# Which engine subtracts the gate weights, when the last quarter loads, and two spare products

## The chip, the cores and the metric

The kernel runs on 1 core of one Trainium2 chip. The metric is device time in microseconds; the runs shown are three executions of the kernel before, with the median as its time.

## The reference, cut to what matters

One decoder layer: 512 tokens, width 1024, all float32. The part that the change touches is the very end, after the mixture of experts:

```python
ffn = _hierarchical_moe(x, ...)                    # per token: two chosen experts
x = _layer_norm(DEEPNORM_ALPHA * x + ffn, ln2_g, ln2_b)
return x + jax.nn.sigmoid(x @ ple_gate_w) * (p_i @ ple_proj_w)
```

`ple_gate_w` is 1024 x 1024, `ple_proj_w` 256 x 1024.

## The kernel before, in words

Each engine has a hand-written program of its own; semaphores order them. A float32 product of full precision is made of three fast ones: weights and activations are each split into a rounded high part (`fp32r`, made by ScalarE with a copy) and the remainder, the low part (a subtraction: raw minus high). TensorE then does high x high, high x low and low x high (`three`, lines 1944 to 1948).

Up to about 560 us the experts run, one item after another: 41 items in all. GpSimd gathers their tokens and scatters their results to DRAM (`pair_dram`). What follows is the epilogue, the functions named `rest` of each engine:

- SyncE (lines 668 to 684) waits until all scattered results have landed, then loads each tile's two rows of expert results ("the pairs", 512 KB for each of tile and choice, `pair_of(t)`), for the four token tiles t of 128, in order, and in between the last two quarters of the gate weights. The gate weights come in four quarters of 1 MB: quarter q holds half `q // 2` of the output columns and half `q % 2` of the contraction. Quarters 0 and 1 are loaded earlier (line 628).
- ScalarE (`rest` from line 1188): rounds quarters 0 and 1 (`round_gate`, line 1161), copies the eight results of the embedding product out of PSUM (`ple_out`, line 1124), rounding quarter 2 after the sixth; waits for two low quarters (line 1195); then for each tile rounds the transposed rows (`turned_high`, line 1200, two halves); rounds quarter 3 after tile 0's; later the sigmoids (line 1207).
- VectorE (`rest` from line 1894): `split_gate(0)` and `split_gate(1)` (line 1858: 128 x 2048 elements, raw minus high); then for each tile t two `expert_sum` (line 1901, result row times its weight plus the residual, 128 x 1024), between them the low parts of the tile before (`turned_low`, line 1602), statistics (line 1577), variance (lines 1583, 1585), `norm_centre` (line 1589) and `norm_scale` (line 1596); `split_gate(2)` after tile 0's scaling and `split_gate(3)` after tile 1's; last the eight products and additions (lines 1934, 1936).
- GpSimd (`rest`, line 895): for each tile `inverse` (line 818), one power of 128 x 1 elements: it waits for the variance, and `norm_scale` waits for it.
- TensorE (`rest` from line 2431): the embedding product (`embed`, line 2228, full float32, 16 products that the profile counts as 32), two spare products whose result nobody reads, the transposition of tile 0 (line 2217, two halves of four), five more spare products, and then the gate products (`gate(t, q)`, 12 fast products for each quarter q and tile t) in the order (0,0) (0,1) (0,2), transposition of tile 1, (0,3) (1,0) (1,1) (1,2), transposition of tile 2, and so on. `gate(0, 0)` needs the first low half of tile 0 (`s_x2lo`); `gate(0, q)` needs the low part of quarter q (`s_glo` at q + 1). The spare products keep TensorE busy; line 2269 is theirs.

Semaphores of the change: `s_ghi` counts rounded quarters, `s_glo` low quarters, `s_quarter[q]` the landing of quarter q, `s_ve2` variances, `s_rs2` inverse roots, `s_ln2` steps of the normalisation, `s_pev` copies of the embedding product, `s_mix` the last products and additions.

Of the kernel before, what the change touches and what calls it, by code (L numbers as in the profile page):

```python
# [4 lines left out]
F32 = mybir.dt.float32  # L5
# [3 lines left out]
ALU = mybir.AluOpType  # L9
# [6 lines left out]
NT, NK = SEQ // P, DM // P  # L16
# [82 lines left out]
def hybrid_layer(nc, d, out, x1_dram, pair_dram):  # L99
    ctx = ExitStack()  # L100
    with ctx:
# [3 lines left out]
        def sem(name):  # L105
            return ctx.enter_context(nc.semaphore(name))
# [51 lines left out]
        bank = [ctx.enter_context(nc.psum_tensor(f"bank{i}", [P, 512], F32)) for i in range(8)]  # L158
# [151 lines left out]
        gate_raw = pieces[SLOTS] + [y_flat[:, 0:GW]]  # L310
        gate_hi = [w_hi[:, GW:2 * GW], w_hi[:, 2 * GW:3 * GW], w_hi[:, 0:GW], last_hi[:, :]]
        gate_lo = [w_lo[:, GW:2 * GW], w_lo[:, 2 * GW:3 * GW], w_lo[:, 0:GW], last_lo[:, :]]
# [5 lines left out]
        def pair_of(t):  # L318

            return raw[:, 2 * GW + t * 2 * DM:2 * GW + (t + 1) * 2 * DM].rearrange("p (k c) -> p k c", k=2)  # L320
# [43 lines left out]
        s_quarter = [sem(f"s_quarter{q}") for q in range(4)]  # L364
# [16 lines left out]
        s_pp, s_pev = sem("s_pp"), sem("s_pev")  # L381
# [13 lines left out]
        s_ghi, s_glo, s_gt = sem("s_ghi"), sem("s_glo"), sem("s_gt")  # L395
        s_r2, s_bn2, s_ve2, s_rs2, s_ln2 = [sem(n) for n in ("s_r2", "s_bn2", "s_ve2", "s_rs2", "s_ln2")]
# [138 lines left out]
        def _(sp):  # L535
# [136 lines left out]
            for t in range(NT):  # L672
                for k in range(2):
                    r = (k * NT + t) * P
                    sp.dma_start(pair_of(t)[:, k, :], pair_dram[r:r + P, :]).then_inc((s_pair, s_xn)[k][t], 16)
                if t == 0:
                    sp.dma_start(gate_raw[2], d["ple_gate"][2, :, :]).then_inc(s_quarter[2], 16)
            sp.dma_start(gate_raw[3], d["ple_gate"][3, :, :]).then_inc(s_quarter[3], 16)
            for u in range(2 * NT):
                t, half = u // 2, u % 2  # L680
                sp.wait_ge(s_mix, 2 * u + 2)
# [5 lines left out]
        def _(pool):  # L687
            g = nc.gpsimd
# [127 lines left out]
            def inverse(t, ready, done):  # L816
                pool.wait_ge(ready, t + 1)
                g.tensor_tensor(rs8[:, t:t + 1], ve8[:, t:t + 1], minus_half[:, 0:1], ALU.pow).then_inc(done, 1)
# [74 lines left out]
                    pool.wait_ge(s_put[s], 4 * PADDED)  # L893

            def rest():
                for t in range(NT):
                    inverse(t, s_ve2, s_rs2)

            expert_blocks(pool, run, fill, rest)

        @block.scalar
# [322 lines left out]
        def _(dve):  # L1224
# [351 lines left out]
            def norm_stats(t, half, count):  # L1576
                v.bn_stats(stat8[:, t, 6 * half:6 * half + 6], mine[:, t, half * 512:(half + 1) * 512])\
                    .then_inc(count, 1)

            def norm_variance(t, count, base, done):  # L1580

                dve.wait_ge(count, base)
                v.bn_aggr(mv8[:, t, :], stat8[:, t, :]).then_inc(count, 1)
                dve.wait_ge(count, base + 1)
                v.tensor_scalar(ve8[:, t:t + 1], mv8[:, t, 1:2], EPS, None, ALU.add).then_inc(done, 1)
# [13 lines left out]
            def turned_low(u, banks, hi, lo):  # L1599
                t, half = u // 2, u % 2  # L1600
                dve.wait_ge(hi, u + 1)
                v.tensor_tensor(a_lo[:, 4 * half:4 * half + 4, t * P:(t + 1) * P],  # L1602
                                banks[u % len(banks)][:, :].rearrange("p (k c) -> p k c", k=4),
                                a_hi[:, 4 * half:4 * half + 4, t * P:(t + 1) * P].bitcast(F32), ALU.subtract)\
                    .then_inc(lo, 1)
# [249 lines left out]

            def split_gate(q):
                dve.wait_ge(s_ghi, q + 1)
                v.tensor_tensor(gate_lo[q], gate_raw[q], gate_hi[q].bitcast(F32), ALU.subtract).then_inc(s_glo, 1)

            def run(b, base, first):  # L1860
# [33 lines left out]
            def rest():  # L1894
                def expert_sum(t, k):
                    if k == 0:
                        dve.wait_ge(s_pair[t], 16)
                    else:
                        dve.wait_ge(s_xn[t], 32)
                    dve.wait_ge(s_r2, NT + 2 * t + k)  # L1900
                    v.scalar_tensor_tensor(out=mine[:, t, :], in0=pair_of(t)[:, k, :], scalar=gate_w[k][:, t:t + 1],
                                           in1=mine[:, t, :], op0=ALU.mult, op1=ALU.add).then_inc(s_r2, 1)

                def expert_variance(t):
                    dve.wait_ge(s_r2, NT + 2 * t + 2)
                    for half in range(2):
                        norm_stats(t, half, s_bn2)
                    norm_variance(t, s_bn2, 3 * t + 2, s_ve2)

                split_gate(0)
                split_gate(1)
                for t in range(NT):
                    expert_sum(t, 0)
                    if t:
                        turned_low(2 * t - 2, turned_2, s_x2hi, s_x2lo)
                        turned_low(2 * t - 1, turned_2, s_x2hi, s_x2lo)
                    expert_sum(t, 1)
                    expert_variance(t)
                    if t == 0:  # L1920
                        dve.wait_ge(s_pev, 4)
                    norm_centre(t, s_ln2)
                    norm_scale(t, s_ln2, s_rs2)
                    if t == 0:
                        split_gate(2)
                    if t == 1:
                        split_gate(3)
                turned_low(2 * NT - 2, turned_2, s_x2hi, s_x2lo)
                turned_low(2 * NT - 1, turned_2, s_x2hi, s_x2lo)
                for u in range(2 * NT):  # L1930
                    t, half = u // 2, u % 2
                    dve.wait_ge(s_sig, u + 1)
                    o = sig[:, t, half * 512:(half + 1) * 512]
                    v.tensor_tensor(o, o, ple_parts[u], ALU.mult).then_inc(s_mix, 1)
                    dve.wait_ge(s_mix, 2 * u + 1)
                    v.tensor_tensor(o, o, mine[:, t, half * 512:(half + 1) * 512], ALU.add).then_inc(s_mix, 1)

            expert_blocks(dve, run, fill, rest)

        @block.tensor  # L1940
        def _(pe):
# [324 lines left out]
            def idle_products(o, m, count):  # L2266

                for _ in range(count):
                    t_.matmul(o[:, :], m[:, 0:P], m, start=True, stop=True)
# [161 lines left out]
            def rest():  # L2431
                pe.wait_ge(s_pr, 32)
                for u in range(2 * NT):
                    embed(u)
                pe.wait_ge(s_glo, 1)
                pe.wait_ge(s_pev, 5)
                idle_products(bank[0], gate_hi[0][:, 0:512], 2)

                def gate(t, q):
                    half, u = q // 2, 2 * t + q // 2  # L2440
                    if half == 0:
                        pe.wait_ge(s_x2lo, 2 * t + 1 + q)
                    if q % 2 == 0:
                        if u < 4:
                            pe.wait_ge(s_pev, 9 + u)
                        else:
                            pe.wait_ge(s_sig, u - 3)
                    pe.wait_ge(s_glo, q + 1)
                    wh, wl = (m[q].rearrange("p (u c) -> p u c", u=4) for m in (gate_hi, gate_lo))
                    for kk in range(4):  # L2450
                        k = 4 * (q % 2) + kk
                        mm = three(gate_bank[u % 4][:, :], a_hi[:, k, t * P:(t + 1) * P], a_lo[:, k, t * P:(t + 1) * P],
                                   wh[:, kk, :], wl[:, kk, :], k == 0, k == NK - 1)
                    if q % 2:
                        mm.then_inc(s_gt, 1)

                for t in range(NT + 1):
                    if t < NT:
                        if t < 2:  # L2460
                            pe.wait_ge(s_pev, 2 * t + 6)
                        pe.wait_ge(s_ln2, 2 * t + 2)
                        turn_tile(t, turned_2, s_x2t, s_x2lo)
                    if t == 0:
                        pe.wait_ge(s_pev, 7)
                        idle_products(bank[2], gate_hi[0][:, 0:512], 5)
                    if t:
                        gate(t - 1, 3)
                    if t < NT:
                        for q in range(3):  # L2470
                            gate(t, q)
# [73 lines left out]
```

## Time and profile before

| | |
|---|---|
| time, median of 3 runs | 636.68 us (635.53 to 638.39) |
| the profiled execution | 636.81 us |
| its span, first to last instruction | 635.1 us |
| mean granted TensorE clock | 0.982 |
| TensorE busy | 601.8 us, 95% |
| VectorE busy | 354.0 us, 56% |
| ScalarE busy | 182.5 us, 29% |
| GpSimd busy | 170.5 us, 27% |

The page gives the busy time of each engine over the whole span. The epilogue, from about 560 us on, is a stretch of its own: the chain of waits and the timeline of each engine tell what sets its length. A timeline row gives the start, the duration and, in square brackets, the idle time before it with what ended it. Rows of like instructions in succession are merged, with their count. A row's start can lie before its engine had the operands: then the duration holds waiting time.

### The profile page before, as it was taken

The numbers are of one execution on the slowest core, as the hardware profiler recorded it, in microseconds if no ns is written. First come the engines' busy times: TensorE is split into PE (matmuls) and PEld (weight loads), VectorE is DVE, ScalarE is ACT, GpSimd is POOL, SyncE is SP. The second block draws the span as 40 slices with busy tenths as digits, with TensorE's granted clock in tenths as the row PEclk, the third lists the DMA queues.
The fourth block names the chain that finished last, engine by engine and source line by source line (L and its number), as shares of the span: only waits on it lengthen the run. The fifth ranks groups of instructions, "written<-read, shape, count | busy, mean of one in ns | idle before, by whom it ended". The sixth has DMA issues, their size and how long they took to land.

```text
span 635.1 us, 11748 instructions
## 1 busy us (share of the span) xinstructions
PE 601.8 (95%) x4575; PEld 434.7 (68%) x4575; DVE 354.0 (56%) x857; ACT 182.5 (29%) x360; POOL 170.5 (27%) x191
## 2 busy tenths in 40 slices
PE   8999999999999999998899999997699999978996
PEld 6768979878888778887665555564355555535885
DVE  6799994788787678869561122221111121139855
ACT  5587324344243245202101111111011111244221
POOL 2428772001010011512032333342234343111100
PEclk9999999999999999999899999997899999989999
DMA  7503241014004002397989999999999999977003
GB/s 245 220 31 145 88 170 62 1 44 156 1 2 166 34 1 68 123 387 274 391 328 343 416 413 418 418 416 417 416 417 418 417 416 416 420 291 315 0 3 135
DMA packets 29285, 149.88 MB, mean 236 GB/s; under 512 B 5992, under 2 KB 6456, under 8 KB 15272
## 3 DMA queue, kind: packets, MB, share of 16 engines
q1 hardware_dynamic: 23624, 140.65, 55.4%
q0 software_dynamic: 5600, 8.42, 3.7%
q8 instruction: 38, 0.62, 0.4%
q14 instruction: 23, 0.19, 0.1%
HBM read 145.23 MB, written 12.98 MB: 249 GB/s over the span
## 4 chain that ended last, share of the span: by engine, by line
PE 74%; DMA 11%; DVE 9%; issue 3%; ACT 1%; POOL 1%; SPq 0%; DVEq 0%; ACTq 0%
PE bank L2319 13%; PE bank L1946 12%; PE bank L1948 12%; PE bank L1947 12%; PE bank L2375 7%; DMA rows_x<-in_ple_gate_dram 5%; DMA slots<-in_w_exp_dram 4%; PE bank L2335 3%; PE bank L2309 2%; PE bank L2051 2%; PE bank L2066 2%; PE bank L2079 2%; PE bank L2352 1%; PE bank L2109 1%; DMA raw<-in_w_in_dram 1%
## 5 line engine op out<-in xcount | busy, mean ns | idle before, releaser
L1848 DVE COPY rows_x<-bank 128x128 f32<-128x128 f32 (+1 forms) x41 | 11.0, 267 | 177.4 <-PE bank L2367 100.3
L1946 PE MATMUL bank<-w_hi,a_hi 128*128 128x384 f32 (+1 forms) x240 | 88.2, 367 | 1.7 <-DVE a_lo L1602 1.7
L1948 PE MATMUL bank<-w_hi,a_lo 128*128 128x384 f32 (+1 forms) x240 | 86.6, 361 | 0.0
L1947 PE MATMUL bank<-w_lo,a_hi 128*128 128x384 f32 (+1 forms) x240 | 86.5, 360 | 0.0
L1946 PE MATMUL bank<-a_hi,w_hi 128*128 128x512 f32 (+1 forms) x168 | 66.5, 396 | 2.7 <-DVE a_lo L1602 1.5
L1947 PE MATMUL bank<-a_lo,w_hi 128*128 128x512 f32 (+1 forms) x168 | 64.5, 384 | 0.0
L1948 PE MATMUL bank<-a_hi,w_lo 128*128 128x512 f32 (+1 forms) x168 | 64.5, 384 | 0.0
L852 POOL DMA_INDIRECT pair_dram<-rows_x,row_put x26 | 26.4, 1015 | 102.4 <-ACT rows_x L1153 102.4
L1946 PEld LDWEIGHTS bank<-w_hi,a_hi 128*128 128x128 f32 x240 | 45.2, 188 | 7.0 <-DVE a_lo L1602 2.1
L1153 ACT ACTIVATE rows_x<-bank 128x512 f32<-128x512 f32 (+1 forms) x41 | 21.3, 520 | 96.0 <-PE bank L2375 74.2
L1948 PEld LDWEIGHTS bank<-w_hi,a_lo 128*128 128x128 f32 x240 | 45.1, 188 | 4.5
L1947 PEld LDWEIGHTS bank<-w_lo,a_hi 128*128 128x128 f32 x240 | 45.1, 188 | 4.3
L2319 PE MATMUL bank<-raw,rows_x 128*64 128x256 f32 x416 | 47.4, 380 | 0.5 <-DVE rows_x L1817 0.5
L2319 PEld LDWEIGHTS bank<-raw,rows_x 128*64 128x64 f32 x416 | 29.6, 137 | 20.3 <-issue 5.5
L1148 ACT ACTIVATE pa<-bank 128x128 f32<-128x128 f32 (+1 forms) x41 | 10.7, 260 | 111.5 <-PE bank L2319 91.0
L1946 PEld LDWEIGHTS bank<-a_hi,w_hi 128*128 128x128 f32 (+1 forms) x168 | 30.7, 183 | 14.0 <-issue 3.0
L1948 PEld LDWEIGHTS bank<-a_hi,w_lo 128*128 128x128 f32 (+1 forms) x168 | 30.6, 182 | 6.4
L1947 PEld LDWEIGHTS bank<-a_lo,w_hi 128*128 128x128 f32 (+1 forms) x168 | 30.7, 183 | 5.5
L752 POOL TENSOR_TENSOR small<-small 128x4 f32<-128x4 f32 x4 | 4.1, 1016 | 113.1 <-DVE small L1463 113.1
L834 POOL DMA_INDIRECT y<-x_dram,row_got x26 | 26.8, 1031 | 26.9 <-DVE row_put L1767 19.3
L716 POOL TENSOR_TENSOR w_lo<-raw,w_hi 128x1024 fp32r<-128x1024 f32 x11 | 26.3, 2401 | 27.5 <-ACT w_hi L910 27.5
L2375 PE MATMUL bank<-raw,rows_x 128*64 128x512 f32 x104 | 26.9, 641 | 5.7 <-issue 5.2
(314 smaller groups left out, 1119.9 us busy)
## 6 DMA issues: line engine op xcount, KB each, us to landing
raw<-in_w_exp_dram SPq DMA_DIRECT2D x45, 1024.0 KB, 19.9
slots<-in_w_exp_dram SPq DMA_DIRECT2D x24, 1024.0 KB, 22.3
pa<-in_w_exp_dram SPq DMA_DIRECT2D x21, 1024.0 KB, 17.8
raw<-in_w_in_dram SPq DMA_DIRECT2D x18, 512.0 KB, 3.6
raw<-in_w_wide_dram SPq DMA_DIRECT2D x4, 1536.0 KB, 7.0
raw<-in_w_out_dram SPq DMA_DIRECT2D x4, 1024.0 KB, 5.9
rows_x<-in_w_exp_dram SPq DMA_DIRECT2D x4, 1024.0 KB, 16.8
raw<-pair_dram SPq DMA_DIRECT2D x8, 512.0 KB, 9.1
```

Of the source, the lines that this page charges most:

```text
L716: g.tensor_tensor(ring(w_lo, i), raw[:, r * PW:(r + 1) * PW], ring(w_hi, i).bitcast(F32), ALU.subtract).then_inc(s_wlo, 1)
L834: g.indirect_dma_start(out=x_got[s], out_offset=None, in_=x1_halves, in_offset=bass.IndirectOffsetOnAxis(ap=row_got[:, c:c + 1], axis=0), ...
L852: g.indirect_dma_start(out=pair_halves, out_offset=bass.IndirectOffsetOnAxis(ap=row_put[:, c:c + 1], axis=0), in_=y_out[s], in_offset=None ...
L1153: a.activation(y_out[s][:, 0:width], bank[4 + s % 2][:, 0:width], ACT.Copy).then_inc(s_outa, 1)
L1946: t_.matmul(o, lh, rh, start=first, stop=False)
L1947: t_.matmul(o, lh, rl, start=False, stop=False)
L1948: return t_.matmul(o, ll, rh, start=False, stop=last)
L2051: mm = t_.matmul(score_bank[hh][:, c0:c1], q_t[rows, g % 2, b * P:(b + 1) * P], k_t[rows, g % 2, c0:c1], start=True, stop=True)
L2066: mm = t_.transpose(o[:, s * P:(s + 1) * P], prob[:, U % 2, s * P:(s + 1) * P], ident[:, :])
L2319: mm = t_.matmul(gu_bank[par][f * SEATS:(f + 1) * SEATS, 0:2 * P], xt[par][:, at_:at_ + SEATS], expert_rows(s, q)[:, c, f * 2 * P:(f + 1) ...
L2335: mm = t_.matmul(o, xt[par][:, at_:at_ + HALF], cols, start=q == 0 and c == 0, stop=q == 1 and c == 3)
L2375: mm = t_.matmul(bank[4 + par][half * SEATS:(half + 1) * SEATS, :], ht[:, f * SEATS:(f + 1) * SEATS], expert_rows(s, 2)[:, 2 * half + f, : ...
```

## The change

Three edits, all in the epilogue.

1. The low parts of quarters 1 and 2 are made by GpSimd instead of VectorE. VectorE keeps quarters 0 and 3. GpSimd's order is: quarter 1, `inverse(0)`, quarter 2, `inverse(1)` to `inverse(3)`. Each subtraction for a quarter q above 0 also waits for `s_glo` to stand at q.
2. SyncE issues the load of quarter 3 behind tile 1's pairs, where it stood behind tile 3's.
3. TensorE's two spare products between the embedding product and the transposition of tile 0 go, with the two waits ahead of them.

```diff
                     sp.dma_start(pair_of(t)[:, k, :], pair_dram[r:r + P, :]).then_inc((s_pair, s_xn)[k][t], 16)
-                if t == 0:
-                    sp.dma_start(gate_raw[2], d["ple_gate"][2, :, :]).then_inc(s_quarter[2], 16)
-            sp.dma_start(gate_raw[3], d["ple_gate"][3, :, :]).then_inc(s_quarter[3], 16)
+                if t < 2:
+                    sp.dma_start(gate_raw[2 + t], d["ple_gate"][2 + t, :, :]).then_inc(s_quarter[2 + t], 16)
...
             def rest():
-                for t in range(NT):
+                def split_gate(q):
+                    pool.wait_ge(s_ghi, q + 1)
+                    pool.wait_ge(s_glo, q)
+                    g.tensor_tensor(gate_lo[q], gate_raw[q], gate_hi[q].bitcast(F32), ALU.subtract).then_inc(s_glo, 1)
+
+                split_gate(1)
+                inverse(0, s_ve2, s_rs2)
+                split_gate(2)
+                for t in range(1, NT):
                     inverse(t, s_ve2, s_rs2)
...
             def split_gate(q):
                 dve.wait_ge(s_ghi, q + 1)
+                if q:
+                    dve.wait_ge(s_glo, q)
                 v.tensor_tensor(gate_lo[q], gate_raw[q], gate_hi[q].bitcast(F32), ALU.subtract).then_inc(s_glo, 1)
...
                 split_gate(0)
-                split_gate(1)
                 for t in range(NT):
                     expert_sum(t, 0)
...
                     norm_scale(t, s_ln2, s_rs2)
-                    if t == 0:
-                        split_gate(2)
                     if t == 1:
                         split_gate(3)
...
                     embed(u)
-                pe.wait_ge(s_glo, 1)
-                pe.wait_ge(s_pev, 5)
-                idle_products(bank[0], gate_hi[0][:, 0:512], 2)
-
                 def gate(t, q):
```

## Rows read from the trace of the kernel before

**Rows 1.** The chain that ended last, 560 to 600 us: start, duration, what.
```profile
537.95 29.63 DMA rows_x<-in_ple_gate_dram
567.60 1.92 ACT w_hi L1161
...
583.25 0.50 PE bank L1946
```
**Rows 2.** Waits of TensorE from 560 us on: total, times, longest.
```profile
PE bank L1946 <- DVE a_lo L1602: 1.7, 1, 1.7
```
**Rows 3.** TensorE in a window: length, busy (instructions), clock, DMA share, GB/s.
```profile
583.30:629.70 46.40, 46.40 (x216) 1.00 0.12 44
```
**Rows 4.** Timeline of VectorE, 565 to 592 us: start, duration, instruction.
```profile
567.18 4.65 DVE L1858 TENSOR_TENSOR w_lo<-rows_x,w_hi 128x2048 fp32r<-128x2048 f32 x2 [8.34 <-ACT w_hi L1161]
571.75 2.68 DVE L1901 SCALAR_TENSOR_TENSOR res<-raw,small,res 128x1024 f32<-128x1024 f32 x2
...
576.11 1.27 DVE L1589 SCALAR_TENSOR_TENSOR res<-res,small,pa 128x1024 f32<-128x1024 f32 x1
577.91 1.29 DVE L1596 SCALAR_TENSOR_TENSOR res<-res,small,pa 128x1024 f32<-128x1024 f32 x1 [0.53 <-POOL small L818]
579.12 2.29 DVE L1858 TENSOR_TENSOR w_lo<-y,w_hi 128x2048 fp32r<-128x2048 f32 x1
...
582.51 1.28 DVE L1602 TENSOR_TENSOR a_lo<-bank,a_hi 128x512 fp32r<-128x512 f32 x2
...
589.65 2.29 DVE L1858 TENSOR_TENSOR last_lo<-y,last_hi 128x2048 fp32r<-128x2048 f32 x1
591.85 1.28 DVE L1901 SCALAR_TENSOR_TENSOR res<-raw,small,res 128x1024 f32<-128x1024 f32 x1
```
**Rows 5.** Timeline of TensorE, 577 to 584 us.
```profile
577.70 1.03 PE L2269 MATMUL bank<-w_hi 128*128 128x512 f32 x2
579.35 1.06 PE L2217 MATMUL bank<-ident,res 128*128 128x128 f32 x8 [0.62 <-DVE res L1596]
580.17 1.39 PE L2269 MATMUL bank<-w_hi 128*128 128x512 f32 x5
```
**Rows 6.** Timeline of ScalarE, 564 to 582 us.
```profile
575.36 1.90 ACT L1161 ACTIVATE w_hi<-y 128x2048 fp32r<-128x2048 f32 x1
...
580.07 1.09 ACT L1200 ACTIVATE a_hi<-bank 128x512 fp32r<-128x512 f32 x2 [1.17 <-PE bank L2217]
```
**Rows 7.** Line 675, the pairs' loads: issues in ns, first and last start, landing.
```profile
L675 SPq DMA_DIRECT2D raw<-pair_dram x8: 335/434/1146, 566.8 to 571.7; - x8
...
DMA to landing us min/median/max: 3.7/9.1/10.9
```
**Rows 8.** Both engines near 252 us and 24 us; lines 1447, 1294: min/median/max ns.
```profile
252.28 4.63 POOL L781 TENSOR_TENSOR w_lo<-raw,w_hi 128x2048 fp32r<-128x2048 f32 x1 [13.83 <-ACT w_hi L1040]
...
253.53 3.41 DVE L1447 SCALAR_TENSOR_TENSOR small<-pa 128x4 f32<-128x4 f32 x1
...
L1447 DVE SCALAR_TENSOR_TENSOR small<-pa x4: 159/161/3407, 147.9 to 253.5; 128x4 f32<-128x4 f32 x4
...
23.70 2.40 POOL L716 TENSOR_TENSOR w_lo<-raw,w_hi 128x1024 fp32r<-128x1024 f32 x1 [2.55 <-ACT w_hi L910]
...
23.77 3.40 DVE L1287 TENSOR_TENSOR_SCAN raw<-raw 4x512 f32<-4x512 f32 x1
...
L1294 DVE TENSOR_TENSOR_SCAN raw<-raw x1: 1204/1204/1204, 32.0 to 32.0; 4x512 f32<-4x512 f32 x1
```
**Rows 9.** GpSimd's first inverse of the epilogue, and its power of line 752.
```profile
576.27 1.54 POOL L818 TENSOR_TENSOR small<-small 128x1 f32<-128x1 f32 x1 [14.10 <-DVE small L1585]
...
L752 POOL TENSOR_TENSOR small<-small x4: 1006/1012/1036, 150.8 to 259.7; 128x4 f32<-128x4 f32 x4
```
**Rows 10.** TensorE after an idle stretch: timeline row, then a window as in Rows 3.
```profile
458.23 3.57 PE L2375 MATMUL bank<-slots,rows_x 128*64 128x512 f32 x8 [5.54 <-issue]
...
458.20:461.40 3.20, 3.17 (x8) 0.50 1.00 417
```

## The prediction

> **What bounds the kernel now.** I read the chain of waits first, then the waits of TensorE in the epilogue, then each engine's timeline there. In the chain the last quarter loaded before the epilogue lands at 567.60, is rounded by ScalarE until 569.52, and then the path runs through VectorE and GpSimd to the first gate product at 583.25 [rows 1]. From there the end is TensorE's alone: from 583.30 to 629.70 it is busy for all 46.40 us, at full clock [rows 3], and its last wait is that 1.7 us for the first low half of tile 0 [rows 2]. What follows 629.7 is ScalarE and VectorE work that the change leaves alone. So the end moves with the start of the gate products, as long as nothing later comes late; the question is what happens to 583.25.
>
> The path to it, on VectorE [rows 4]: two quarters split, 567.18 to 571.83; two expert sums to 574.43; statistics and variance; centring from 576.11 to 577.38; GpSimd's inverse from 576.27 to 577.81 [rows 9]; scaling from 577.91 to 579.20; quarter 2 split; the next tile's first sum; the first low half from 582.51, 0.74 us ahead of the gate product. TensorE's transposition begins at 579.35, 0.15 after the scaling, ScalarE's rounding of its first half at 580.07, and the five spare products end at 581.56 [rows 5, 6].
>
> **On paper, a gain.** VectorE loses one split of 2.3 us ahead of the sums and one behind the scaling [rows 4]. The first pair is issued at 566.8 and lands after 3.7 us, at 570.5 [rows 7], so the sums could begin 1.25 us earlier than 571.75, not 2.3. The transposition then starts at about 578.15, its first half is rounded by 579.55, and without the second split VectorE is free for the low half at 579.6: first gate product at 580.35 to 580.4, a gain of 2.85 us. That is what the edit is worth if GpSimd's splits disturb nobody.
>
> **What GpSimd's split does to VectorE.** At 252.28 GpSimd made the low part of a quarter of w_out: same operation, same 128 x 2048, 4.63 us, until 256.91. VectorE's line 1447, a scalar_tensor_tensor with both inputs in SBUF, began at 253.53 and took 3.41 us, where three of its like took about 0.16; it ended at 256.94. At 23.70 GpSimd held 2.40 us, until 26.10; VectorE's scan, begun 0.07 us later, took 3.40 us where the other scan took 1.20 [rows 8]. In both cases VectorE's instruction ran as though it had started 0.13 us before GpSimd's record ended. So a GpSimd subtraction that has begun holds back a VectorE instruction with two SBUF inputs for its whole length. The other way round it looks the same: each inverse begins 0.16 us after a centring, ends 0.43 us after it, and takes 1.54 us for one column, while the power of four columns took 1.01 us [rows 4, 9]. Expert sums, centring and scaling all have two SBUF inputs; the statistics have one, the low halves one and one in PSUM.
>
> The Trainium skill, "SBUF — State Buffer", section "Who interferes with whom", says this outright: a VectorE instruction with two SBUF inputs contends with a GpSimd instruction that reads SBUF, and whichever starts first makes the other wait for its whole length. By that rule the trace agrees, and the change has the effect of the main case below; the sum on paper would need it to be false.
>
> **Part by part.**
> - Split 1 on GpSimd. ScalarE's rounding ends at 569.5, so GpSimd starts at about 569.58 and, at 4.63 us, ends at 574.21 [rows 1, 8]. The first pair lands at 570.5, a microsecond behind, so the sum finds GpSimd at work and runs from 574.08. Two sums at 2.68 us end at 576.76 instead of 574.43 [rows 4]: +2.33 us. Centring runs from 578.44, the inverse from 578.60 to 580.14.
> - Split 2 on GpSimd. Quarter 2 is rounded at 577.26 [rows 6], so when the inverse ends nothing holds the subtraction back. VectorE's scaling follows the inverse by 0.10 us (577.81 to 577.91) [rows 4, 9]. GpSimd needs no message from another engine: I take its start as 580.10, before the scaling's. Then it ends at 584.73 and the scaling runs from 584.60 to 585.89, where it ended at 579.20: +6.69 us. Queued behind the scaling on VectorE are tile 1's first sum and the low halves; on TensorE everything waits for it.
> - Split 2 gone from VectorE. Behind the scaling only the sum (1.28 us) stands ahead of the low half: 587.1. TensorE transposes at 586.04; the rounding of the first half would end at 587.4, the low half begin there, and the gate product at 588.15; the five spare products end 2.21 us after the transposition began, 588.25. So at full clock 588.3: +5.0 us.
> - The clock. TensorE idles from 577.7 to 586.0, 8.3 us. After 5.54 us of idling the granted clock was 0.50 from the restart at 458.23 to 461.4 [rows 10]. If the restart at 586.0 meets the same, some 3.2 us at half speed lie over the transposition and the spare products, and cost 1.5 us (between 0, and 1.7 with all of it lost): gate products from 589.8, **+6.55 us**.
> - The two spare products. They ran from 577.70 to 578.73, in a gap that ended at 579.35 [rows 5]: their removal frees nothing. It lengthens the idle time by 1 us out of 8, so I price it at 0, at most the clock's 1.7, already counted.
> - The load of quarter 3. VectorE needs it at 589.65 at the earliest, behind tile 1's scaling; having it sooner gives 0. The pairs of tiles 2 and 3 come one quarter later. From 570.5 to 571.7 + 10.9 = 582.6 seven more of their loads and quarter 2, of twice the size, landed [rows 7], 1.34 us for each 512 KB; quarter 3 ahead adds 2.7 us, so the last pair is there by 585.3, against 591.85 for tile 2's first sum [rows 4]. Price 0, and the cover grows as the chain moves later.
> - Later splits and tiles. Nothing else of GpSimd's is long. Split 3 stays on VectorE and keeps its place relative to the gates. ScalarE's wait for two low quarters is over at 574.2, before its first rounding. Quarter 2's low part, at 584.7, is before gate(0, 2) at 589.8 + 5.5. Price 0.
>
> **Sum.** 635.1 + 6.55 = 641.65 us of span; with the 1.7 us around the span (636.81 against 635.1), 643.4; the profiled run lies 0.13 above the median, so 643.2 against 636.68, 1.0% slower.
>
> **Rivals.**
> 1. GpSimd's splits disturb nobody (the hold applies to other forms only). For it: rows 8 show small VectorE instructions, none of 128 x 1024. Against: line 1447 is the very operation of the sums. Time 636.7 - 2.85 = 633.8, 0.45% faster. It decides if expert sums keep their 1.28 us under GpSimd's split. Chance 0.13.
> 2. The first hold is right, but VectorE's scaling gets ahead of split 2. Scaling 580.25 to 581.5, transposition at 581.65; split 2 then goes between the scaling and tile 1's sum, until 586.1, and the sum, with the low half behind it, ends at 587.3: gate at 588.05, +4.8 us: 641.5. Spare products are over by then even at half clock. Chance 0.15.
> 3. GpSimd comes late to its epilogue, since its branch follows the last scatter's landing (566.8) and its next work before was at 576.27 [rows 9], so nothing shows it ready at 569.6. If it starts between 570.6 and 571.8, the first sum gets through, the second waits until 576.4, and its end is 0.9 us later than in the main case: 644.1. Later still adds as much again, 645. Chance 0.08.
> 4. The change does nothing measurable, hold and gain in balance. Only if GpSimd holds once, for the first sums: +2.33, -2.3 for the second split, with a microsecond for the clock: 636.7 to 637.7. Chance 0.04.
>
> The main case has 0.60, within it the clock's part from 0 to 1.7 (641.7 to 643.4).
>
> **How the numbers follow.** The likeliest is the main case, 643.2. The range reaches over the main case and rivals 2 and 3, about 0.83: 641.0 to 645.2. About 0.5% (3.2 us) is what a measurement can tell from no change: rival 1 lies just inside it, so it is shared, 0.06 faster and 0.07 same, with 0.04 for rival 4; slower by over 0.5% holds 0.83.
>
> **What would show each step.** In the profile after: the first expert sum with a duration of about 4.8 us, ending at 575.4 with GpSimd's first split; the first scaling some 5.6 us long, ending with the second; TensorE's idle time of 8 us for the scaling ahead of line 2217, a clock of 0.5 behind it; the gate products without a gap from about 589.8. An expert sum of 1.28 us at 570.5 would prove the main case wrong, and so would a scaling of 1.29 us right behind the inverse (rival 2, if the next sum is long instead).

## The result and the profile after

The changed kernel takes 642.37 us (median of 6 runs, 641.37 to 644.23) against 636.36 us before (6 runs, 635.51 to 638.39): 0.96% slower, ratio 1.0096 with a 95% interval of 1.0076 to 1.0117. The forecast was 643.2 us and a ratio of 1.0102. The profiled execution took 642.17 us, its span is 640.4 us and its mean granted clock 0.981. Among all executions reported below, one stands apart, 3343.66 us for the kernel before with six spare products, and it is left out of that version's ratio.

VectorE's timeline from 560 to 600 us in the kernel after (start, duration, instruction, idle time before it), to be laid beside [rows 4]:

```profile
565.79 2.29 DVE L1867 TENSOR_TENSOR w_lo<-rows_x,w_hi 128x2048 fp32r<-128x2048 f32 x1 [6.78 <-ACT w_hi L1168]
570.40 5.12 DVE L1910 SCALAR_TENSOR_TENSOR res<-raw,small,res 128x1024 f32<-128x1024 f32 x2 [2.32 <-DMA raw<-pair_dram]
...
577.19 1.27 DVE L1596 SCALAR_TENSOR_TENSOR res<-res,small,pa 128x1024 f32<-128x1024 f32 x1
579.00 5.46 DVE L1603 SCALAR_TENSOR_TENSOR res<-res,small,pa 128x1024 f32<-128x1024 f32 x1 [0.53 <-POOL small L817]
584.38 1.27 DVE L1910 SCALAR_TENSOR_TENSOR res<-raw,small,res 128x1024 f32<-128x1024 f32 x1
586.41 1.49 DVE L1609 TENSOR_TENSOR a_lo<-bank,a_hi 128x512 fp32r<-128x512 f32 x2 [0.76 <-ACT a_hi L1207]
...
593.75 2.29 DVE L1867 TENSOR_TENSOR last_lo<-y,last_hi 128x2048 fp32r<-128x2048 f32 x1
```

And GpSimd's, beside [rows 9]:

```profile
568.52 4.52 POOL L898 TENSOR_TENSOR w_lo<-rows_x,w_hi 128x2048 fp32r<-128x2048 f32 x1 [6.17 <-ACT w_hi L1168]
577.35 1.54 POOL L817 TENSOR_TENSOR small<-small 128x1 f32<-128x1 f32 x1 [4.31 <-DVE small L1592]
578.88 4.49 POOL L898 TENSOR_TENSOR w_lo<-y,w_hi 128x2048 fp32r<-128x2048 f32 x1
```

Both holds are to be read off. The two sums took 5.12 us together instead of 2.68. They ended at 575.52, as though the first had run from 572.84, 0.20 us before the end of GpSimd's record (573.04). The scaling took 5.46 us instead of 1.29 and ended at 584.46, as though it had run from 583.17, again 0.20 us before the end of GpSimd's record (583.37). Between the inverse's end (578.89) and the scaling's start lay 0.11 us, and by then GpSimd had begun (578.88).

TensorE's timeline, beside [rows 5], its waits as in [rows 2], and three windows of it with columns as in [rows 3]:

```profile
561.45 14.00 PE L2234 MATMUL bank<-pa 128*128 128x512 f32 x32 [1.31 <-DMA pa<-in_ple_proj_dram]
584.60 1.94 PE L2223 MATMUL bank<-ident,res 128*128 128x128 f32 x8 [9.15 <-DVE res L1603]
586.19 2.48 PE L2275 MATMUL bank<-w_hi 128*128 128x512 f32 x5
588.47 0.63 PE L1952 MATMUL bank<-w_hi,a_hi 128*128 128x512 f32 x1
...
PE bank L2223 <- DVE res L1603: 9.2, 1, 9.2
...
579.20:584.40 5.20, 0.00 (x0) 0.50 0.86 347
584.60:588.90 4.30, 4.30 (x15) 0.50 0.02 6
590.00:634.80 44.80, 44.80 (x210) 1.00 0.11 42
```

### The profile page after: what moved, and what is told of

It is laid out like the page before. It is cut to its first block, busy times and chain, and to the rows that moved or that the text cites. A ratio compares the mean times of both kernels' runs of the same rounds, so it can differ in the third digit from the quotient of the medians.

```text
span 640.4 us, 11746 instructions
## 1 busy us (share of the span) xinstructions
PE 600.3 (94%) x4573; PEld 434.7 (68%) x4573; DVE 356.6 (56%) x855; ACT 182.3 (28%) x360; POOL 179.7 (28%) x193
## 4 chain that ended last, share of the span: by engine, by line
PE 77%; DMA 10%; DVE 7%; issue 3%; POOL 1%; ACT 1%; SPq 0%; ACTq 0%; DVEq 0%; POOLq 0%
PE bank L1952 13%; PE bank L2325 13%; PE bank L1953 13%; PE bank L1954 13%; PE bank L2381 7%; DMA rows_x<-in_ple_gate_dram 5%; DMA slots<-in_w_exp_dram 4%; PE bank L2341 3%; PE bank L2315 2%; PE bank L2057 2%; PE bank L2072 2%; PE bank L2085 2%; PE bank L2358 1%; PE bank L2275 1%; PE bank L2115 1%
## 5 line engine op out<-in xcount | busy, mean ns | idle before, releaser
L2325 PE MATMUL bank<-raw,rows_x 128*64 128x256 f32 x416 | 48.7, 388 | 0.5 <-DVE rows_x L1824 0.5
```

What stands on the lines that cost most here:

```text
L2325: mm = t_.matmul(gu_bank[par][f * SEATS:(f + 1) * SEATS, 0:2 * P], xt[par][:, at_:at_ + SEATS], expert_rows(s, q)[:, c, f * 2 * P:(f + 1) ...
```

## The experiments

Theory A: a GpSimd subtraction that has begun holds back any VectorE instruction with two SBUF inputs until it is over. Rival B: nothing is held; the work on GpSimd merely delays what is queued on GpSimd, or the cause lies in the other two edits. The experiments ran in three groups, each with runs of the kernel before on the same chip; comparisons across groups go by their ratios.

### GpSimd's second subtraction alone

Quarter 1 back on VectorE:

```diff
                 split_gate(0)
+                split_gate(1)
                 for t in range(NT):
...
-                split_gate(1)
                 inverse(0, s_ve2, s_rs2)
                 split_gate(2)
```

> The changed kernel with quarter 1's low part back on VectorE; GpSimd makes only quarter 2's. Theory A (a GpSimd subtraction that has begun holds back a VectorE instruction with two SBUF inputs): the expert sums are undisturbed (1.28 us each), the first scaling is recorded at about 5.4 us and ends 4.3 us later than in the kernel before, TensorE restarts cold at half clock after some 6 us of idling, gate products about 4.1 us later than before: 640.5 us. Rival B (nothing is held; GpSimd's work only delays what is queued behind it on GpSimd): the inverse stands ahead of this split, so nothing is late, and VectorE is free of one split: the gate products come up to 1.7 us earlier than before, 634.7 us, scaling 1.29 us.

Measured: 640.83 us, ratio 1.0078 (1.0053 to 1.0104). VectorE's timeline of this kernel:

```profile
570.94 2.68 DVE L1909 SCALAR_TENSOR_TENSOR res<-raw,small,res 128x1024 f32<-128x1024 f32 x2
...
577.10 5.46 DVE L1602 SCALAR_TENSOR_TENSOR res<-res,small,pa 128x1024 f32<-128x1024 f32 x1 [0.54 <-POOL small L817]
```

The sums are undisturbed, the scaling is held exactly as in the changed kernel. Rival B, as far as it speaks of GpSimd's queue, had this kernel faster than before; that part falls.

### GpSimd's first subtraction alone

Quarter 2 back on VectorE, behind tile 0's scaling; quarter 1 stays on GpSimd:

```diff
                     norm_scale(t, s_ln2, s_rs2)
+                    if t == 0:
+                        split_gate(2)
...
                 inverse(0, s_ve2, s_rs2)
-                split_gate(2)
```

> The changed kernel with quarter 2's low part back on VectorE; GpSimd makes only quarter 1's. Theory A: the first expert sum is held until GpSimd's record ends (two sums together about 5.1 us), the chain is 1.1 to 2.3 us later than before, the scaling takes 1.29 us, and TensorE idles 3 to 4 us, so that part of the restart is at half clock: 637.5 to 639 us. Rival B: the sums start with the first pair at 570.4 and take 2.68 us together, 1.2 us ahead of before: 635.2 us.

Measured: 639.95 us, ratio 1.0065 (1.0040 to 1.0089). VectorE and GpSimd in this kernel:

```profile
570.02 6.08 DVE L1909 SCALAR_TENSOR_TENSOR res<-raw,small,res 128x1024 f32<-128x1024 f32 x2 [1.07 <-DMA raw<-pair_dram]
...
579.58 1.28 DVE L1602 SCALAR_TENSOR_TENSOR res<-res,small,pa 128x1024 f32<-128x1024 f32 x1 [0.53 <-POOL small L817]
...
569.10 4.51 POOL L898 TENSOR_TENSOR w_lo<-rows_x,w_hi 128x2048 fp32r<-128x2048 f32 x1 [7.53 <-ACT w_hi L1167]
```

The first sum is held until GpSimd's record ends at 573.61, and the scaling is not held: theory A's pattern. But the size is above what I expected, 4.1 us over before instead of 1 to 2.5. In the profiled execution the sums end 1.7 us later than in [rows 4], and the transposition took 1.94 us at half clock; that execution took 638.2 us, the fastest of the ten. The ten executions give a hint: the three slowest, 641.67 to 642.22 us, have a mean granted clock of 0.975, the two fastest, 638.2 and 638.28, of 0.983 and 0.984. So the rest goes with a lower clock; what lowers it in some executions, and where, no trace shows, and it stays open.

### No subtraction on GpSimd, the other two edits kept

Both on VectorE, in the places of the kernel before:

```diff
                 split_gate(0)
+                split_gate(1)
...
+                    if t == 0:
+                        split_gate(2)
...
-                split_gate(1)
-                inverse(0, s_ve2, s_rs2)
-                split_gate(2)
-                for t in range(1, NT):
+                for t in range(NT):
                     inverse(t, s_ve2, s_rs2)
```

> All four low parts on VectorE as in the kernel before; the earlier load of quarter 3 and the removal of the two spare products kept. Priced at 0 each: 636.4 us, the same as before within 0.5 us. A rival in which the removal of the two products is what cools TensorE gives half clock after a gap that was 0.6 us and is now 1.7 us: up to 1.7 us more, 638 us.

Measured: 636.55 us, ratio 0.9998 (0.9965 to 1.0031). The earlier load and the removed products together cost or bring nothing within 0.35%. So the loss of 0.96% comes from the subtractions on GpSimd, and the part of rival B that blames the other two edits falls too. Nothing in the median does not mean nothing in the trace: in the profiled execution TensorE idled 2.8 us ahead of the transposition, the clock was at 0.50 from about 578.6 to 585.4, and the gate products, begun at 581.56, 1.7 us ahead of [rows 1], ended no sooner than in the kernel before. Whether the two removed products would have kept the clock up there, no trace shows.

### GpSimd busy, but only writing

The low parts of quarters 1 and 2 are left out; memsets of zeros stand in their places:

```diff
-                    g.tensor_tensor(gate_lo[q], gate_raw[q], gate_hi[q].bitcast(F32), ALU.subtract).then_inc(s_glo, 1)
+                    for c in range(0, GW, 48):
+                        ins = g.memset(gate_lo[q][:, c:min(c + 48, GW)].bitcast(F32), 0.0)
+                    ins.then_inc(s_glo, 1)
```

> The changed kernel with each GpSimd subtraction replaced by 43 memsets of 48 columns into the same tile (the low parts of quarters 1 and 2 are left out and stand at zero), so that GpSimd is busy for about as long, 4 to 5 us, in the same places, but reads nothing of SBUF. Theory A, in the form that only GpSimd's reads hold VectorE's second input: sums 1.28 us each from 570.4, scaling 1.29 us, gate products 2.5 to 2.9 us earlier than before: 633.8 us. If any GpSimd work holds VectorE, or if the cause is GpSimd's queue: as the changed kernel, 642 us.

Measured: 634.25 us, ratio 0.9969 (0.9944 to 0.9993). The memsets took 3.2 us in each place, less than the 4 to 5 I meant, but they lie over what was held. GpSimd and VectorE in this kernel:

```profile
568.48 3.20 POOL L899 MEMSET w_lo<- 128x48 f32 x43 [5.94 <-ACT w_hi L1170]
...
577.17 3.21 POOL L899 MEMSET w_lo<- 128x48 f32 x43 [0.63 <-ACT w_hi L1170]
...
570.49 2.68 DVE L1912 SCALAR_TENSOR_TENSOR res<-raw,small,res 128x1024 f32<-128x1024 f32 x2 [2.37 <-DMA raw<-pair_dram]
...
576.65 1.28 DVE L1605 SCALAR_TENSOR_TENSOR res<-res,small,pa 128x1024 f32<-128x1024 f32 x1 [0.53 <-POOL small L817]
577.85 1.28 DVE L1912 SCALAR_TENSOR_TENSOR res<-raw,small,res 128x1024 f32<-128x1024 f32 x1
```

The first sum begins at 570.49 while GpSimd writes until 571.68, and tile 1's first sum at 577.85 while GpSimd writes from 577.17 on. Both take their usual time. So it is not enough that GpSimd works. One caution: the memsets are 43 short instructions and not one long one, so a hold of one instruction each could delay a sum by little. But the hold works in the other direction too (see the run started after the scaling), so the sums would have held the memsets in turn, and they didn't: in the 1.17 us from 577.93, with the sum running, the profile has 18 memsets, and in the 1.18 us from 579.20, without it, 17. What of the subtraction makes the hold, that it reads SBUF at all or that it reads two operands, these runs don't separate. This run is also about what the change would bring if there were no hold: 0.3%, where the prediction had 0.45% on paper; its GpSimd work is 1.3 us shorter in each place.

### The subtraction in four pieces

```diff
-                    g.tensor_tensor(gate_lo[q], gate_raw[q], gate_hi[q].bitcast(F32), ALU.subtract).then_inc(s_glo, 1)
+                    for c in range(0, GW, 512):
+                        ins = g.tensor_tensor(gate_lo[q][:, c:c + 512], gate_raw[q][:, c:c + 512],
+                                              gate_hi[q][:, c:c + 512].bitcast(F32), ALU.subtract)
+                    ins.then_inc(s_glo, 1)
```

> The changed kernel with each GpSimd subtraction cut into four of 512 columns (about 1.2 us each, so 5 us in all). Theory A with the hold as long as one instruction: each VectorE instruction with two SBUF inputs waits for at most one piece and then gets its turn, so the longest sum or scaling is about 2.5 us instead of 5.4; three or four such waits of up to 1.2 us on the path, less than in the changed kernel: 638 to 640 us. If the holder keeps its right from one piece to the next (pieces queued back to back), as the changed kernel: 642 us, first scaling over 5 us.

Measured: 637.62 us, ratio 1.0034 (0.9990 to 1.0077). VectorE and GpSimd in this kernel:

```profile
572.37 4.19 DVE L1913 SCALAR_TENSOR_TENSOR res<-raw,small,res 128x1024 f32<-128x1024 f32 x2 [2.07 <-DMA raw<-pair_dram]
...
580.03 2.23 DVE L1606 SCALAR_TENSOR_TENSOR res<-res,small,pa 128x1024 f32<-128x1024 f32 x1 [0.53 <-POOL small L817]
582.18 2.30 DVE L1913 SCALAR_TENSOR_TENSOR res<-raw,small,res 128x1024 f32<-128x1024 f32 x1
584.40 1.27 DVE L1612 TENSOR_TENSOR a_lo<-bank,a_hi 128x512 fp32r<-128x512 f32 x2
585.60 2.36 DVE L1913 SCALAR_TENSOR_TENSOR res<-raw,small,res 128x1024 f32<-128x1024 f32 x1
...
570.77 6.92 POOL L899 TENSOR_TENSOR w_lo<-rows_x,w_hi 128x512 fp32r<-128x512 f32 x4 [6.84 <-ACT w_hi L1171]
...
579.91 6.96 POOL L899 TENSOR_TENSOR w_lo<-y,w_hi 128x512 fp32r<-128x512 f32 x4
```

The hold lasts one instruction: the scaling and tile 1's two sums each wait for one piece, about 1 us, and then have their turn, although the next piece stands queued. GpSimd in its turn waits between pieces: four take 6.9 us, where whole ones took 4.5. The low halves, with one SBUF input, take 1.27 us for two as ever, in the midst of the pieces. By the ratios about two thirds of the loss is gone, though the interval reaches from a fifth of it to all. It came out slightly below what I expected.

### The two spare products kept

```diff
                     embed(u)
+                pe.wait_ge(s_glo, 1)
+                pe.wait_ge(s_pev, 5)
+                idle_products(bank[0], gate_hi[0][:, 0:512], 2)
```

> The changed kernel with the two spare products and their waits put back. TensorE idles some 9 us ahead of the transposition; two products take 1 us of it off its beginning, and the clock has fallen long before the restart either way: 642.4 us, the same as the changed kernel within 0.5 us. A rival in which the products keep the clock up would show the transposition at 1.06 instead of 1.94 us and 640.8 us.

Measured: 643.49 us, ratio 1.0103 (1.0074 to 1.0131): 1.1 us above what I expected, but by the ratio the changed kernel's 1.0096 within the intervals. TensorE's restart:

```profile
584.17 1.94 PE L2223 MATMUL bank<-ident,res 128*128 128x128 f32 x8 [6.94 <-DVE res L1603]
```

The transposition took 1.94 us here too, after 6.9 us of waiting for the scaling.

### The same subtraction, started after the scaling

The kernel with GpSimd's second subtraction alone, and one wait more:

```diff
                 inverse(0, s_ve2, s_rs2)
+                pool.wait_ge(s_ln2, 2)
                 split_gate(2)
```

> Quarter 1's low part on VectorE, quarter 2's on GpSimd in one piece as in the run with GpSimd's second split alone, but GpSimd waits for the end of tile 0's scaling before it starts. Same work on the same engines, one wait more. Theory A: scaling 1.29 us, the hold falls on tile 1's second sum (about 4 us), where there is slack of 2 us; gate products 2 to 2.9 us earlier than in the kernel before, some 1.5 us of it given back when tile 1's transposition and quarter 3 come late: 634.5 to 636 us. If the cause were the work on GpSimd and not its place, as that other run: 640.8 us.

Measured: 637.63 us, ratio 1.0035 (0.9994 to 1.0076), 1.6 us above the upper end of what I expected, but 0.43% below the run without the wait (1.0078; the two intervals overlap, 1.0053 against 1.0076, so the trace carries this point). VectorE and GpSimd:

```profile
576.48 1.28 DVE L1603 SCALAR_TENSOR_TENSOR res<-res,small,pa 128x1024 f32<-128x1024 f32 x1 [0.53 <-POOL small L817]
577.68 1.28 DVE L1910 SCALAR_TENSOR_TENSOR res<-raw,small,res 128x1024 f32<-128x1024 f32 x1
579.26 1.29 DVE L1609 TENSOR_TENSOR a_lo<-bank,a_hi 128x512 fp32r<-128x512 f32 x2 [0.30 <-ACT a_hi L1207]
580.47 4.03 DVE L1910 SCALAR_TENSOR_TENSOR res<-raw,small,res 128x1024 f32<-128x1024 f32 x1
...
577.84 5.56 POOL L898 TENSOR_TENSOR w_lo<-y,w_hi 128x2048 fp32r<-128x2048 f32 x1 [1.47 <-DVE res L1603]
```

Same work, same engines; only the place of the hold has moved, to tile 1's second sum (4.03 us), where TensorE is at work on gate products. And the other direction shows: this time VectorE's sum had begun first (577.68), and GpSimd's subtraction, begun 0.16 us later, took 5.56 us instead of 4.5. The profiled execution took 636.07 us; there quarter 3's low part came 0.7 us late for TensorE, and the clock fell to half some 0.7 us after the restart behind a gap of 2.8 us. The ten executions spread from 635.72 to 644.58 us, and again the slow end has the lower clock: 0.974 and 0.976 for the two slowest, 0.985 to 0.989 for the four fastest.

### GpSimd only where VectorE reads SBUF once

A version meant to beat both. The two spare products are kept, quarters 0, 1 and 3 are VectorE's; quarter 2's 2048 columns are shared out, and the waits on `s_glo` for quarters 2 and 3 count one more. `part(a, b)` subtracts columns a to b of quarter 2; `s_r2` counts the expert sums, and the two waits are for tile 1's first and second, so that the first part starts when VectorE turns to the low halves and the second when it turns to the statistics:

```diff
                 inverse(0, s_ve2, s_rs2)
-                split_gate(2)
+                pool.wait_ge(s_ghi, 3)
+                pool.wait_ge(s_r2, NT + 3)
+                part(0, 640)
+                pool.wait_ge(s_r2, NT + 4)
+                pool.wait_ge(s_glo, 3)
+                part(640, 1280).then_inc(s_glo, 1)
...
                         turned_low(2 * t - 1, turned_2, s_x2hi, s_x2lo)
+                    if t == 1:
+                        dve.wait_ge(s_ghi, 3)
+                        v.tensor_tensor(gate_lo[2][:, 1280:GW], gate_raw[2][:, 1280:GW],
+                                        gate_hi[2][:, 1280:GW].bitcast(F32), ALU.subtract).then_inc(s_glo, 1)
                     expert_sum(t, 1)
```

> A version meant to be faster than both. Spare products kept, quarters 0, 1 and 3 on VectorE; quarter 2's low part: columns 0 to 640 on GpSimd while VectorE makes tile 0's low halves (one SBUF input each), columns 640 to 1280 on GpSimd during tile 1's statistics, 1280 to 2048 on VectorE behind the low halves. Theory A: no VectorE instruction is held for more than 0.3 us, gate products about 1.8 to 2.5 us earlier than before, TensorE without a gap behind them: 634 us. If GpSimd's reads hold the low halves and the statistics too, each is recorded at up to 1.4 us more, and the time is as before, 636 us.

Measured: 635.59 us, ratio 0.9988 (0.9955 to 1.0020), 1.6 us above what I expected. VectorE and GpSimd:

```profile
578.13 1.28 DVE L1913 SCALAR_TENSOR_TENSOR res<-raw,small,res 128x1024 f32<-128x1024 f32 x1
579.71 1.29 DVE L1612 TENSOR_TENSOR a_lo<-bank,a_hi 128x512 fp32r<-128x512 f32 x2 [0.30 <-ACT a_hi L1210]
580.92 1.03 DVE L1932 TENSOR_TENSOR w_lo<-y,w_hi 128x768 fp32r<-128x768 f32 x1
581.88 1.27 DVE L1913 SCALAR_TENSOR_TENSOR res<-raw,small,res 128x1024 f32<-128x1024 f32 x1
583.18 1.29 DVE L1587 BATCH_NORM_STATS2 small<-res 128x6 f32<-128x512 f32 x2
...
579.56 1.58 POOL L896 TENSOR_TENSOR w_lo<-y,w_hi 128x640 fp32r<-128x640 f32 x1 [2.73 <-DVE res L1913]
583.23 1.58 POOL L896 TENSOR_TENSOR w_lo<-y,w_hi 128x640 fp32r<-128x640 f32 x1 [2.09 <-DVE res L1913]
```

The low halves and the statistics take their usual 1.29 us for two with GpSimd's subtractions on top of them: theory A's last prediction, that instructions with one SBUF input are free of it, holds.

### How many spare products

Left over was the half clock after short gaps. Theory C says that spare products which close the gap ahead of tile 0's transposition gain time; rival D that they don't. The version above with six, with none, and the kernel before with six:

```diff
-                idle_products(bank[0], gate_hi[0][:, 0:512], 2)
+                idle_products(bank[0], gate_hi[0][:, 0:512], 6)
```

> The version with GpSimd's work in the two windows, with six spare products ahead of tile 0's transposition instead of two. Theory C (the granted clock falls when TensorE idles 2 to 3 us ahead of the transposition, which it does in the executions where the embedding product runs at full clock, 14.0 us instead of 15.7): four more products, 1 us, close that gap, so the gate products start at full clock in every execution; where the embedding product took 15.7 us they cost at most 0.2 us. 634.9 us, 0.7 below two products, with less spread. Rival D (the spare products don't matter at this length of gap): the same as with two, 635.6 us.

> The same version with no spare products ahead of the transposition, as in the changed kernel. Theory C: the gap is 1 us longer in every execution, more of the executions restart at half clock, up to 1.7 us each: 636.3 us, and more spread. Rival D: 635.6 us.

> The kernel before with six spare products instead of two, nothing else. Theory C: executions with a fast embedding product gain up to 1.5 us, those with a slow one lose nothing (its gap is 0.6 us, and the four products take 1 us, so 0.4 us at most): 635.0 us, 0.1% faster than before. Rival D: 0 to 0.4 us slower.

Measured: six, 634.48 us, ratio 0.9968 (0.9943 to 0.9993); none, 634.41 us, 0.9972 (0.9957 to 0.9987); the kernel before with six, 636.24 us, 0.9991 (0.9966 to 1.0017). The granted clock in the profiled executions, with none and then with six (windows, columns as in [rows 3]):

```profile
579.00:581.00 2.00, 0.42 (x2) 0.81 0.97 406
581.00:583.00 2.00, 2.00 (x10) 0.50 1.02 414
...
579.00:581.00 2.00, 2.00 (x15) 1.00 1.02 416
581.00:583.00 2.00, 2.00 (x10) 1.00 1.02 406
```

With none, the clock fell to half behind a gap of 2.8 us; with six there was neither a gap nor half clock. But the two executions differ in more than the spare products: the embedding product took 14.0 us with none and 15.7 us with six, which by itself takes 1.7 us of the time ahead of the transposition, and the version with two, profiled with 15.7 us as well, idled 0.6 us and kept the full clock too. Nearer to a test is the kernel before with six, profiled with 14.0 us: it idled 1.4 us and kept 1.00. Nor does the gap alone decide. The clock fell behind gaps of 2.6 to 2.8 us in four kernels (with 14.0 us each), yet the kernel with the pieces idled 3.25 us, after 15.6 us of embedding product, and kept 1.00 through the gap and the restart.

In time, theory C had six and none 1.4 us apart, and their medians are equal to 0.1 us: as a forecast of time it falls. Rival D fits better, though both versions came out 1.1 us below its 635.6; the kernel before with six came out where D had it, but its interval holds C's 0.1% too. The two traces are also poor samples: with none, the profiled execution (637.36 us) was the slowest of its twelve, with six (635.93 us) the second slowest. Why the clock seen in them doesn't show in the medians is open. Both versions are 0.3% faster than the kernel before and, by the ratios, 1.3% faster than the changed one; that they beat the version with two spare products (0.9988, up to 1.0020) is not shown.

## Why the prediction was right, step by step

- **What bounds it.** Right. The gate products' start moved by 5.2 us and the span by 5.3. Between the medians the difference is 6.0 us, where the forecast had 6.5.
- **The hold.** Right in both places, in its rule (the one that has begun keeps the other out), and in its restriction to two SBUF inputs, which the prediction took from two small instructions [rows 8]; here it is shown for 128 x 1024, and against memsets, pieces and instructions with one input. The overlap with the end of GpSimd's record is 0.20 us here, where the prediction had 0.13.
- **Split 1.** Start 568.52 instead of 569.58, since quarter 1 was rounded a microsecond sooner in this execution (from 566.52, against 567.60 in [rows 1]); 4.52 us instead of 4.63. So the sums ended 1.09 us later than in [rows 4], not 2.33. Nearly all of that 1.2 us is the earlier rounding and not the hold. In [rows 1] and [rows 4] the sums end 6.83 us after that rounding begins; counted so, in this execution they would have ended at 573.35 without the change (an estimate from these rows), and they ended at 575.52: the hold cost 2.2 us. The size of the term was right; what I had taken as fixed was one execution's start. In the runs with both early quarters on VectorE the first sum began anywhere from 570.07 to 573.20, against 571.75 in [rows 4].
- **Split 2.** The race behind the inverse went as argued, by 0.1 us, and did so in each of the profiled executions with that order. The scaling took 5.46 us and ended 5.26 us later than before (6.69 expected); of the 1.43 us between, 1.24 are split 1's, and most of the rest is that this subtraction took 4.49 us instead of 4.63.
- **The clock.** Half clock at the restart, as expected. From the transposition to the first gate product it took 3.87 us, where I had 3.76. At full clock the five spare products end 2.21 us after the transposition begins [rows 5], so the clock cost about 1.7 us here, an estimate, where 1.5 was priced. That equals what the split taken off VectorE gave back: in the kernel before the same stretch took 3.90 us, because the low half stood behind that split. The half clock lasted 4.7 us from the restart, longer than the 3.2 us assumed from [rows 10].
- **Spare products and load.** 0 together, as priced (ratio 0.9998 with both edits alone, give or take 0.3%), and 0 for the products (1.0103 with them kept against 1.0096). The load was not run by itself.
- **Sum.** +5.2 us instead of +6.55 in the profiled execution, most of it the earlier start named under split 1; the median of 642.37 us lies 0.8 below the forecast, the ratio 0.0006. That the median came so close is in part luck, since one execution's start, which scatters by some 3 us, stood for all. Rival 1 (633.8 us) is close to what the write-only run shows in the absence of the hold, 634.25. Rival 2's order was made by hand with the wait for the scaling; there VectorE's next sum was not caught, since it followed the scaling without a gap. So rival 2's price, with that sum held, would have been too high.

## What to carry to other kernels

Work moved to GpSimd is not free for VectorE when both read SBUF: before moving an elementwise step, look in the trace for VectorE instructions with two SBUF inputs in its shadow, and count what is left of the GpSimd instruction as their delay if they are on the path (4.2 us of 4.5 for the scaling here). Let such a step start where VectorE reads PSUM or one operand, or cut it into pieces; one wait that changes only where it starts took the hold off the path here (scaling 1.28 instead of 5.46 us). In the race behind the inverse, the instruction that is ready in its queue won against the one on the other engine that waited for a semaphore from it: GpSimd's subtraction began 0.11 to 0.12 us before the scaling in all four traces with this order.

## What the runs showed of the hardware that I had not expected

- The two engines take turns: with pieces of 512 columns VectorE had its turn after each piece (2.23, 2.30 and 2.36 us for instructions of 1.28), and GpSimd's four pieces stretched to 6.9 us.
- GpSimd's memsets of 48 columns came one every 75 ns (3.20 us for 43); they held nobody, and no VectorE instruction held them.
- The embedding product takes 14.0 us in some executions and 15.7 in others, for the same 32 instructions. In the slow one of the kernel before the clock fell to half some 1.4 us after it began, behind 2.6 us of idling; in those of 14.0 us the idle time ahead was 1.1 to 2.3 us; one execution with 1.8 us took 15.6, so the gap alone doesn't decide. In every trace it was over before tile 0's scaling ended, so its own length did not set TensorE's restart.
